# Expert cells: VectorE loads the tile's number earlier and frees PSUM later, ScalarE copies the next input ahead of the turned rows

## What is computed

```python
comb = (one_hot(gsel, N_GROUPS)[:, :, None] * w_grp[:, None, :] * gw[:, :, None]).reshape(T, N_EXPERTS)
y = jnp.zeros_like(t)
for e in range(N_EXPERTS):                       # 16 experts, 2 chosen per token
    he = jax.nn.silu(t @ exp_w1[e]) * (t @ exp_w3[e])      # 1024 -> 256
    y = y + comb[:, e:e + 1] * (he @ exp_w2[e])            # 256 -> 1024
```

## Time and profile before

| | us |
|---|---|
| median of 3 runs | 2216.7 (2214.8 to 2218.0) |
| the profiled execution | 2218.13 |
| its span, first to last instruction | 2216.3 |
| first cell's first matmul to the last cell's mark (L1167) | about 541 to 768 |
| busy: TensorE, weight loads, VectorE, ScalarE | 2094.1, 1661.2, 1455.1, 987.0 |
| mean granted clock of TensorE | 0.979 |

### The profile page before, as it was taken

The page is one execution under the profiler, slowest core; times in us unless marked ns, Lnnn a source line. Parts: engine busy times, 40 slices in busy tenths (PEclk is TensorE's granted clock), DMA queues, the critical chain, the costliest instruction groups (busy, mean ns, idle before and its releaser), DMA issues.

```text
span 2216.3 us, 29664 instructions
## 1 busy us (share of the span) xinstructions
PE 2094.1 (94%) x9758; PEld 1661.2 (75%) x9758; DVE 1455.1 (66%) x2421; ACT 987.0 (45%) x1646; POOL 11.1 (1%) x25
## 2 busy tenths in 40 slices
PE   5989999978999889989999999999999999999997
PEld 5978888867666567766666788888877777888885
DVE  6884444563888866566765788883466758888633
ACT  3345333443676632536665433333345744333321
POOL 0000000001000000000000000000000000000000
PEclk9999999978999999989999999999999999999998
DMA  4220132222999615210000222323320022333332
GB/s 152 92 59 1 55 91 94 94 65 82 333 319 325 228 43 156 72 48 1 1 1 29 87 95 94 95 95 108 102 85 29 0 62 91 95 95 95 96 108 81
DMA packets 61144, 213.48 MB, mean 96 GB/s; under 512 B 8048, under 2 KB 9200, under 8 KB 60928
## 3 DMA queue, kind: packets, MB, share of 16 engines
q1 hardware_dynamic: 59792, 210.73, 29.0%
q10 hardware_dynamic: 1264, 1.61, 0.3%
HBM read 209.03 MB, written 2.10 MB: 95 GB/s over the span
## 4 chain that ended last, share of the span: by engine, by line
PE 79%; DVE 13%; ACT 3%; issue 3%; DMA 0%; DVEq 0%; SPq 0%; ACTq 0%
PE psum L810 57%; PE psum L941 2%; PE psum L1381 2%; DVE sig L2440 2%; PE psum L1208 2%; PE psum L964 2%; DVE w_lo_more L2164 2%; PE psum L981 1%; PE psum L980 1%; PE psum L1149 1%; DVE w_lo L2164 1%; DVE y_slots L2705 1%; DVE w_lo L2177 1%; PE psum L1317 1%; PE psum L1364 1%
## 5 line engine op out<-in xcount | busy, mean ns | idle before, releaser
L810 PE MATMUL psum<-x_hi,w_hi 128*128 128x512 f32 (+1 forms) x1440 | 519.0, 378 | 16.7 <-DVE x_lo L2211 6.6
L810 PE MATMUL psum<-x_lo,w_hi 128*128 128x512 f32 (+1 forms) x1440 | 513.5, 374 | 0.0
L810 PE MATMUL psum<-x_hi,w_lo 128*128 128x512 f32 (+1 forms) x1440 | 510.8, 372 | 0.0
L2177 DVE TENSOR_TENSOR w_lo<-raw,w_hi 128x1024 fp32r<-128x1024 f32 x243 | 296.0, 1221 | 190.7 <-ACT w_hi L1507 190.1
L1507 ACT ACTIVATE w_hi<-raw 128x1024 fp32r<-128x1024 f32 x243 | 255.5, 1054 | 178.5 <-DMA raw<-stream 178.3
L810 PEld LDWEIGHTS psum<-x_hi,w_hi 128*128 128x128 f32 x1440 | 262.8, 189 | 74.5 <-issue 11.4
L810 PEld LDWEIGHTS psum<-x_lo,w_hi 128*128 128x128 f32 x1440 | 262.0, 189 | 53.0 <-issue 4.1
L810 PEld LDWEIGHTS psum<-x_hi,w_lo 128*128 128x128 f32 x1440 | 262.7, 190 | 48.7
L810 PE MATMUL psum<-hid_hi,w_hi 128*128 128x512 f32 x624 | 245.2, 393 | 3.9 <-issue 3.2
L810 PE MATMUL psum<-hid_lo,w_hi 128*128 128x512 f32 x624 | 245.3, 393 | 0.0
L810 PE MATMUL psum<-hid_hi,w_lo 128*128 128x512 f32 x624 | 244.4, 392 | 0.0
(11 more groups left out here) (537 smaller groups left out, 3222.2 us busy)
## 6 DMA issues: line engine op xcount, KB each, us to landing
raw<-stream SPq DMA_DIRECT2D x251, 512.0 KB, 3.5
raw<-experts SPq DMA_DIRECT2D x70, 512.0 KB, 5.1
raw_more<-experts SPq DMA_DIRECT2D x68, 512.0 KB, 5.1
resid<-x_fm SPq DMA_DIRECT2D x4, 528.0 KB, 7.0
out_fm<-resid SPq DMA_DIRECT2D x4, 512.0 KB, 2.9
consts<-consts_in SPq DMA_DIRECT2D x1, 1373.0 KB, 13.9
kv_pairs<-kv_even_odd ACTq DMA_DIRECT2D x4, 256.0 KB, 4.1
inv_count<-inv_counts SPq DMA_DIRECT2D x1, 528.0 KB, 11.4
```

The source lines that it names most:

```text
L810: last = pe.matmul(o, wt[:, slot, k * P:(k + 1) * P], m[part], start=start and p == 0, stop=stop and p == 2, skip_group_check=True)
L2177: dve.tensor_tensor(w_lo[:, slot, :], raw[:, slot, :], w_hi[:, slot, :].bitcast(F32), ALU.subtract)\
```

## The change

ScalarE: `hidden_hi(c - 1)` moves behind `cell_input(c + 1)`. VectorE: the load of the tile's number leaves `cell_input` for a function `find_tile`, called ahead of `hidden_lo(c - 1)`; `freed(c - 1)` moves behind `cell_input(c + 1)`; the wait and the release at the end of `output_add` become `output_freed`, called behind the next low part. After the last cell, `output_freed` follows each `output_add` directly. The computation, the tiles in memory and SyncE's and TensorE's programs are the same.

```diff
@@ ScalarE @@
                 if c:
                     moe_high(6 * c + 1)
                     moe_high(6 * c + 2)
-                    hidden_hi(c - 1)
                 if c + 1 < CELLS:
                     cell_input(c + 1)
+                if c:
+                    hidden_hi(c - 1)
@@ VectorE @@
             def cell_input(c):
-                tile = 0
-                if c:
-                    tile = tile_of[c] = dve.value_load(WALK[0:1, 0, c:c + 1], min_val=0, max_val=TILES - 1)
                 dve.wait_ge(x_hi_ready, c + 1)
-                dve.tensor_tensor(XC[c % 2][:, 1, :], XG[:, :, :].rearrange("p k n -> p (k n)")[:, bass.ds(tile * D, D)],
+                dve.tensor_tensor(XC[c % 2][:, 1, :], XG[:, :, :].rearrange("p k n -> p (k n)")[:, bass.ds(tile_of[c] * D, D)],
                                   XC[c % 2][:, 0, :].bitcast(F32), ALU.subtract).then_inc(cell_x, 1)
+
+            def find_tile(c):
+                tile_of[c] = dve.value_load(WALK[0:1, 0, c:c + 1], min_val=0, max_val=TILES - 1)
...
                 dve.tensor_tensor(y, y, pair(output_result(c)).rearrange("p a n -> p (a n)"), ALU.add).then_inc(y_added, 1)
+
+            def output_freed(c):
                 dve.wait_ge(y_added, c + 1)
                 dve.sem_inc(lin_free, 1)
...
                     moe_low(6 * c + 2)
+                if c + 1 < CELLS:
+                    find_tile(c + 1)
+                if c:
                     hidden_lo(c - 1)
-                    freed(c - 1)
                 if c + 1 < CELLS:
                     cell_input(c + 1)
                 if c:
+                    freed(c - 1)
                     moe_low(6 * c + 3)
                     moe_low(6 * c + 4)
                 if c > 1:
                     output_add(c - 2)
                 if c:
                     moe_low(6 * c + 5)
+                if c > 1:
+                    output_freed(c - 2)
                 hidden_gate(c)
...
             output_add(CELLS - 2)
+            output_freed(CELLS - 2)
             output_lo(TILES - 2)
             output_add(CELLS - 1)
+            output_freed(CELLS - 1)
```

## The result

The changed kernel takes **2196.16 us** (median of 6 runs, 2194.03 to 2197.44) against 2217.21 us for the kernel before (6 runs, 2214.82 to 2227.06): a ratio of 0.9904, with a 95% interval of 0.9894 to 0.9915, about 21 us less. The forecast was 2199.0, its range 2196.5 to 2208.0. The time is faster, as forecast, and lies 0.34 us under the low end of the range: the gain was 3 us larger than worked out.

The account below looks back on a forecast made before the run. The prediction took a circle of waits through ScalarE, VectorE and TensorE as the bound. Gains of 12.9 us (regular cells) and 5.8 (late cells) less 1.0 (transfers) made 17.7 us: 2199.0 us, range 2196.5 to 2208.0.

Parts of the forecast that it names:

- the two waits: Ahead of VectorE's subtraction, 0.95 us: ScalarE's copy and VectorE's own queue end almost together; moving either alone gives about 0.04 us.
- Part 1, the copy: ScalarE's 1.06 us copy of the next input fits in its 3.01 us idle time before the turned rows: cost 0.
- Part 2, the load: VectorE's load of the tile's number hides under low parts: cost 0, or 0.73 us a cell if unhidden.
- Part 3, the releases: VectorE frees PSUM later: 0.24 us a cell saved behind its addition; the hidden pair's later release costs 0.
- The new sum, regular cells: TensorE becomes the bound at 9.01 us a cell; 16 cells take 144.2 instead of 157.0 us, gaining 12.9 us.
- Late cells: Last four cells, where VectorE also makes output low parts: VectorE bounds at 9.67 us a cell, gaining 5.8 us.
- The DMA engines: Weight transfers, late next: full queue's 367 GB/s would allow 8.57 us a cell; single slow ones lose 1.0 us in all.
- the sign that the prediction gave for rival B: ScalarE waiting for raw transfers, or landings above 6.5 us, would mean that transfers bound the cells.
- rival B: Transfers become the bound in regular cells at 9.3 us a cell (338 GB/s): 2202.6 us; chance 12%.
- A: VectorE's load is not hidden and waits until VectorE has drained: 10.9 us gained, 2205.8 us; chance 12%.
- C: One of the two waits stays in another form: only 5 us gained, 2212 us, or nothing; chance 4%.
- D: Slower: a late-landing unit delays ScalarE's high part and copy, pushing back the turned rows: 10 us lost, 2227; chance 2%.

Follow-up runs that it names:

- Copy alone: Kernel before with only ScalarE's copy of the next input moved ahead of the turned rows: ratio 0.9994, regular cells 9.78 us from mark to mark.
- load alone: Kernel before with only VectorE's load of the tile's number moved ahead: ratio 0.9989, marks 9.82 us apart in regular cells, 10.30 in late ones.
- releases alone: Kernel before with only VectorE's two PSUM releases moved later: ratio 0.9974, marks 9.58 us apart in regular cells, 9.68 in late ones.
- copy and load together: Changed kernel with both PSUM releases put back to their old places: 2202.55 us, ratio 0.9928, regular cells 9.16 us from mark to mark.
- repeated run: The changed kernel measured once more without any edit: 2196.78 us (7 runs), ratio 0.9895 to the kernel before.
- run 15: Not a run's number: 15 counts late transfers that ScalarE met when the changed kernel was measured again without any edit, 2196.78 us.
- run with less work: Changed kernel without the product of the input's low part, so less work for TensorE and VectorE: 2175.51 us in one run.
- doubled load: Changed kernel with VectorE's load of the tile's number made twice in a row: 2194.48 us in one run, marks 8.85 and 9.67.

## Why the prediction came out as it did

**What bounds the kernel before.** Right: the two waits lie beside each other. Copy alone 9.78, load alone 9.82 and both 9.16 show that in the regular cells each hid the other. In the late cells the copy was early already, and the load alone gave 0.62 us.

**Part 1, the copy.** Right, cost 0: ScalarE still waits 1.7 us for the turned rows, and its output copy in the late cells fits, the late marks being VectorE's own 9.67.

**Part 2, the load.** Right, cost 0 in this place. The trace shows the load start under the gate, and a second load is free as well. This is also what the Trainium skill says in Advanced Engine Details and Errata, section Sequencer and Instruction Queues, of control instructions; the runs add the condition, that the queue must not stand at a wait just ahead.

**Part 3, the releases.** The price of 0.24 us was right (releases alone: 9.82 to 9.58). The hidden pair's release, which the prediction treated only for whom it might hold up, has a price too: 0.36 us a cell, where the prediction's 0.91 less 0.73 had left 0.18 for it. It is the larger part of the 0.6 us that copy and load together leave on VectorE.

**The new sum, regular cells.** Here the step failed that reads "9.01 us, which is its own time for a cell". That TensorE becomes the bound was right; its own time is 8.85. The cell that served as its measure, cell 1 to 2, had a hidden wait of 0.16 us for the low part of the split output unit. The table of waits gives it no releaser and files it under issue, and I took that for there being none. 16 cells at 0.16 us are 2.5 us, and 0.16 more came from the mark of cell 2 being read from another view: measured 15.55 where the term was 12.9. The trace of before would have shown it: TensorE's weight loads for L1181 come 0.43 us apart, and the first of L1191 came 0.90 us behind the last of them. Of these 0.47 us more, 0.16 reached the marks.

**Late cells.** Right to 0.1 us: 9.66 against 9.67, 5.76 against 5.8, with TensorE's stall ahead of the fourth unit where it was expected (0.50 us for about 0.7).

**The DMA engines.** This is the second term that was mis-sized. I took a loss of 1.0 us for single slow transfers; the marks are 8.85 or 8.86 in every cell, so the loss is 0. ScalarE does meet late transfers: five in the whole stage, 1.5 us in all, and in the repeated run 15, 4.2 us in all, with landings up to 7.2 us. In neither does a mark move, so the sign that the prediction gave for rival B (ScalarE waiting for transfers, or landings above 6.5 us) shows late transfers and not that they bound. The limit was too low as well: 391 GB/s in the run with less work. The Trainium skill, DMA: Bandwidth & Descriptors, section Specifications, gives about 358 GB/s for a core, as half of what two cores share; the 355 GB/s of the changed kernel looks like that ceiling, but here one core works alone, and the 391 measured show that it was none.

**The sum.** 2.6 us from the regular cells, 1.0 from the transfers and 0.2 in the first cell make the 3.8 us by which the stage's 21.5 us exceed the 17.7 predicted; the median gained 21.05. The lower end of the range, 2196.5, had been put by the scatter of medians and a DMA loss of 0, with nothing for an error in TensorE's time, though it was read from one cell. On which side of that end the median fell is chance, though: the same kernel came to 2196.16 and, when repeated, to 2196.78 us. What does not hang on chance is the distance of the marks, 8.85 where 9.01 stood. One sum of the chances is off too: the forecast, A, B and half of C make 0.96, not 0.94.

**The rivals.** A (the load not hidden) falls with the row of the load and with the doubled load. B (transfers) falls at 9.3 us; its place is at 8.05 or below. C falls for the change as a whole: no wait took the place of the removed ones. It is what happens to the copy alone and to the load alone. D falls: transfers landed within 6.3 us (7.2 in the repeated run), and no cell was longer than before.

## What to carry to other kernels

When two waits end together, removing one changes only the releaser's name: look for the second (an engine's own completion, or its queue) before putting a price on the first, and time each part by a distance of marks rather than by the whole. On VectorE's queue a register load was free or not according to what wait stood ahead of it, so try loads ahead of waits, and releases of an engine's own work behind its next large instruction. And before an engine's time is used as the next bound, check the cell that it is read from for gaps without a releaser: compare each distance with its like in the same rows.

## What the runs showed of the hardware

- GpSimd's work slowed VectorE by more than the work moved: beside a subtraction of 128x1024 fp32 on GpSimd (2.40 us), two of VectorE's took 4.33 us instead of 2.35. Moving 1.13 us of work to the idle engine cost 0.85 us a cell.
- With loads of 512 KB one core moved 391 GB/s over 123 us, where the fullest stretch read before had 367; landing then took 5.8 us in the middle, 7.0 at most.
- A release that has to wait for its own engine's last result costs that engine 0.36 us behind a short subtraction (0.29 us lasting) and 0.24 us behind an addition of 1.22 us; the same release behind the next large instruction added nothing to VectorE's cell (9.67 us in the late cells, the sum of its own work).
- A wait of TensorE's queue can be unseen in the profile: behind an fp32 matmul, whose modelled end covers it, a wait of 0.16 us stood as "issue".
